# Stage o of an eight-stage network on one core: each block's product with the values issued one step later, with its transposed weights in two buffers

## The reference, cut to what matters

```python
def block(i, qb):
    sc = jnp.einsum('bqhd,bkhd->bhqk', qb, k, preferred_element_type=f32) * scale
    p = jax.nn.softmax(jnp.where(chunk_causal_mask(i, s), sc, -jnp.inf), axis=-1)
    return jnp.einsum('bhqk,bkhd->bqhd', p.astype(v.dtype), v)
```

## Time and profile before

| | us |
|---|---|
| median of 3 runs | 3006.23 |
| lowest, highest | 3006.18, 3006.42 |
| profiled execution, its own time | 3008.05 |
| its span | 3006.3 |
| PE busy in it | 2913.7 (97%) |
| DVE busy | 1715.1 (57%) |
| ACT busy | 1061.7 (35%) |
| weight transfers | 456 of 512 KB |

### The profile page before, as it was taken

One profiled execution on the slowest core, in us unless ns is written; L12 is line 12 of the kernel. 1 busy time (PEld: TensorE's weight loads), 2 busy tenths in 40 slices (PEclk: granted clock), 3 DMA queues, 4 the chain that ended last, 5 costly groups with the idle time before them and its releaser, 6 DMA issues.

```text
span 3006.3 us, 38676 instructions
## 1 busy us (share of the span) xinstructions
PE 2913.7 (97%) x14206; PEld 2406.5 (80%) x14206; DVE 1715.1 (57%) x2639; ACT 1061.7 (35%) x1601; POOL 211.6 (7%) x256
## 2 busy tenths in 40 slices
PE   8999999999999999999999999989999988999998
PEld 6888888888888888878888876588888875788887
DVE  5554535765577666654455586656444576464445
ACT  4332323543354432233332324343232345442222
POOL 1000000000000100000000000015511110110001
PEclk9999999999999999999999999989999999999999
DMA  4322232122212233333222331113332310223332
GB/s 147 98 93 89 91 106 78 57 57 78 84 57 64 70 107 98 93 97 97 92 91 91 91 99 43 29 57 113 98 95 87 105 57 22 64 84 98 93 96 91
DMA packets 70400, 252.14 MB, mean 84 GB/s; under 512 B 7808, under 2 KB 9856, under 8 KB 69632
## 3 DMA queue, kind: packets, MB, share of 16 engines
q1 hardware_dynamic: 68112, 241.89, 26.4%
q10 hardware_dynamic: 2016, 7.96, 0.8%
q0 software_dynamic: 144, 0.52, 0.0%
HBM read 248.25 MB, written 2.10 MB: 83 GB/s over the span
## 4 chain that ended last, share of the span: by engine, by line
PE 85%; DVE 8%; ACT 4%; issue 3%; POOL 1%; DMA 0%; DVEq 0%; ACTq 0%; POOLq 0%
PE ps L297 18%; PE ps L299 17%; PE ps L298 17%; PE ps L568 2%; PE ps L569 2%; PE ps L570 2%; ACT w_high L277 2%; DVE w_low L284 2%; PE ps L782 1%; PE ps L784 1%; PE ps L783 1%; PE ps L1809 1%; PE ps L855 1%; PE ps L591 1%; PE ps L841 1%
## 5 line engine op out<-in xcount | busy, mean ns | idle before, releaser
L284 DVE TENSOR_TENSOR w_low<-raw,w_high 128x1024 fp32r<-128x1024 f32 x456 | 566.4, 1247 | 417.4 <-ACT w_high L277 410.3
L297 PE MATMUL ps<-h_high,w_high 128*128 128x512 f32 x1872 | 737.1, 394 | 3.4 <-DVE arena L969 1.7
L299 PE MATMUL ps<-h_high,w_low 128*128 128x512 f32 x1872 | 729.7, 390 | 0.0
L298 PE MATMUL ps<-h_low,w_high 128*128 128x512 f32 x1872 | 729.2, 390 | 0.0
L277 ACT ACTIVATE w_high<-raw 128x1024 fp32r<-128x1024 f32 x456 | 477.9, 1051 | 448.6 <-PE ps L299 204.2
L297 PEld LDWEIGHTS ps<-h_high,w_high 128*128 128x128 f32 x1872 | 352.1, 188 | 75.1 <-DVE arena L969 2.5
L299 PEld LDWEIGHTS ps<-h_high,w_low 128*128 128x128 f32 x1872 | 351.7, 188 | 73.7
L298 PEld LDWEIGHTS ps<-h_low,w_high 128*128 128x128 f32 x1872 | 352.0, 188 | 69.7
L297 PE MATMUL ps<-y_high,w_high 128*128 128x512 f32 x640 | 250.4, 391 | 0.6 <-DVE y_low L1944 0.2
L298 PE MATMUL ps<-y_low,w_high 128*128 128x512 f32 x640 | 249.1, 389 | 0.0
L299 PE MATMUL ps<-y_high,w_low 128*128 128x512 f32 x640 | 249.0, 389 | 0.0
(11 more groups left out here) (443 smaller groups left out, 4511.0 us busy)
## 6 DMA issues: line engine op xcount, KB each, us to landing
raw<-stream SPq DMA_DIRECT2D x456, 512.0 KB, 3.6
table<-tables_in ACTq DMA_DIRECT2D x5, 1088.0 KB, 6.4
x<-x_in ACTq DMA_DIRECT2D x8, 256.0 KB, 8.3
x_out<-x SPq DMA_DIRECT2D x16, 128.0 KB, 1.7
const<-const_in SPq DMA_DIRECT2D x1, 673.0 KB, 8.0
arena<-ssm_in POOLq DMA_DIRECT2D x1, 512.0 KB, 5.9
params<-params_in ACTq DMA_DIRECT2D x1, 287.0 KB, 6.7
```

The costliest lines, as they stand in the source:

```text
L284: nc.vector.tensor_tensor(w_low[:, u.slot], raw[:, u.raw], w_high[:, u.slot].bitcast(F32), ALU.subtract).then_inc(weights_low, 1)
L297: nc.tensor.matmul(bank, wh, high[:, k], start=k == 0, stop=False)
L298: nc.tensor.matmul(bank, wh, low[:, k], start=False, stop=False)
L299: mm = nc.tensor.matmul(bank, wl, high[:, k], start=False, stop=k == tiles - 1)
```

## The change

`o_step` now gives v = n - 4, so a block's product comes one step later, and there are 28 steps instead of 27. `o_wt` becomes a pair: even blocks (128 or 384 columns) go to a region of 384 columns in the constants (the last 128 columns of the mask `chunk` and two rotation matrices), odd blocks (256 or 512 columns) to the place used before. ACT's copy of block n - 2 now waits for the product of block n - 4 (`o_pv` at tr - 1). PE's transposition of block n - 2 gets an explicit wait for ACT's copy of block n - 3 (`o_wt_copied` at tr), because bank 6 is still single. With v, the head's end moves too: `y_high` on ACT and `y_low` on DVE come one step later, in the steps with n = 4h + 7 instead of 4h + 6 for head h.

```diff
-        O_STEPS = NBLK * MLA_HEADS + 3
+        O_STEPS = NBLK * MLA_HEADS + 4
...
-        o_wt = work[:, 0:T]
+        o_wt = (con("chunk", 3 * P, 3 * P), work[:, 0:T])
...
-            s, w, t, v = (m if 0 <= m < O_BLOCKS else None for m in (n, n - 1, n - 2, n - 3))
+            s, w, t, v = (m if 0 <= m < O_BLOCKS else None for m in (n, n - 1, n - 2, n - 4))
...
                         for kb in range(b + 1):
                             mm = nc.tensor.matmul(ps[:, o_pv_bank(h), b * P:(b + 1) * P], o_v[:, kb, h * P:(h + 1) * P],
-                                                  o_wt[:, kb * P:(kb + 1) * P], start=kb == 0, stop=kb == b)
+                                                  o_wt[v % 2][:, kb * P:(kb + 1) * P], start=kb == 0, stop=kb == b)
                         mm.then_inc(o_pv, 1)
                     if tr is not None:
                         pe.wait_ge(o_scaled, tr + 1)
+                        if tr > 0:
+                            pe.wait_ge(o_wt_copied, tr)
...
-                        if tr > 0:
-                            act.wait_ge(o_pv, tr)
-                        nc.scalar.activation(o_wt[:, 0:width], ps[:, 6, 0:width], ACT.Copy).then_inc(o_wt_copied, 1)
+                        if tr > 1:
+                            act.wait_ge(o_pv, tr - 1)
+                        nc.scalar.activation(o_wt[tr % 2][:, 0:width], ps[:, 6, 0:width], ACT.Copy).then_inc(o_wt_copied, 1)
```

## The result

The kernel before took 3006.37 us in the median of 8 runs (3006.18 to 3008.39), the changed kernel 3016.11 us in the median of 8 (3013.66 to 3020.00). The ratio is 1.0032, with an interval of 1.0021 to 1.0042: slower by 0.3%, or 9.7 us. The forecast was 3007.6 us, its range ended at 3010.6, and a loss above 3012.2 had a chance of 0.03. The prediction was wrong.

A forecast was written before the change was run, and what follows sets the result against it. PE's chain of waits (85%) was taken as the bound, so only time PE loses can be won; eight nonzero or zero terms and a ninth of 0 summed to +1.42 us on 3006.23, giving 3007.6 us, range 3003.6 to 3010.6.

The forecast's parts named there:

- term 3: Step 10: DVE's `y_low` goes to step 11, so block 11's mask starts earlier: -0.33 us, bounds 0 and -0.68.
- the first rival: PE's waits for ACT's copy really go, transpositions follow earlier: in full 2998.3 us (chance 0.02), in part 3003.7 (0.26).
- term 7: Steps 22 and 23: three groups replace four at the low clock, -0.44, then four replace one, +0.67: +0.23 us.
- 1, up to `cy`: Step 3 loses block 0's product, for whose scores DVE waited; products of steps 4 to 6 lie in pauses: -0.22 us.
- 2, block 3 behind `cy`: Block 3's four groups leave the pause ahead of `cy` for step 7, where one group stood: +0.67 us.
- 4, steps 12 to 17: Pauses ended by the exponential, squares, tanh and scaling; products of any size fit into them: 0.
- 5, behind `glu`: Steps 18 and 19 follow `glu` without a pause; 3 + 4 groups where 4 + 1 stood: +0.45 us.
- 6, `y_low` at the gate: The fourth head's `y_low` comes directly ahead of the gate's tiles and delays block 19's inverse: +0.62 us, bounds 0 and +0.68.
- 8, the end: Last transposition starts slightly earlier, last product waits for ACT's copy as before: 0, at best -0.1 us.
- a rival with 0.20: PE's clock falls to low at `cy` or `glu`: one 3009.8 us (0.15); both 3012.1 (twice or with more, 0.05).
- a sign of being wrong: A granted clock of 0.50 where it was 1.00, or the reverse, would show the forecast wrong; no size given.
- The rival that a fall goes away: The mostly low-clock 7.5 us from 2559.11 shrink by at most 3.3 us: 3004.3; not expected, no separate chance given.

The follow-up runs named there:

- warm kernels: The orders before and after the change, both with unread matmuls in PE's pauses: before_warm 3004.67 us and after_warm 3006.04 us.
- before_warm: Kernel before plus unread matmuls in PE's pauses (7 ahead of `cy`; 3, 3, 6 in steps 13, 17, 21): 3004.67 us, ratio 0.9987.
- after_warm: Changed kernel plus unread matmuls in PE's pauses (7 ahead of `cy`; 5, 5, 10 in steps 13, 17, 21): 3006.04 us, ratio 0.9992.
- cy_ahead: Changed kernel with block 3's product put back into the pause ahead of `cy`: 3012.08 us, ratio 1.0008 to before.
- fill_cy: Changed kernel plus 7 unread matmuls ahead of `cy` only: 3011.76 us, ratio 1.0011 to before.
- after_again: Changed kernel run once more, unaltered, beside the kernel before: 3016.36 us, ratio 1.0021.
- behind_cy: Kernel before with the buffer pair and only block 3's product, with head 0's `y_high` and `y_low`, moved to step 7: 3013.18 us, ratio 1.0010.
- before_warm2: before_warm0 plus 2 unread matmuls in step 2 and 5 in step 25: 3000.91 us, ratio 0.9971 to the kernel before.
- before_warm0: before_warm plus 8 unread matmuls ahead of the scores of step 0: 3004.28 us, ratio 0.9987 to the kernel before.

## Why the prediction was wrong

**The waits.** Right. They moved from the products to the transpositions, 12.7 us to 1.3 and 3.9 to 13.9 of weight loads. Counted from the scores of its own block, in the warm kernels, a transposition came 0.14 to 0.23 us earlier for blocks 3, 4, 8, 12, 16, 20 and 23, and 0.60 for block 10, which `y_low` no longer holds (term 3). For the others it came at the same time or up to 0.66 later, and in sum nothing is won: the first rival is refuted. The page's rule "Double-buffer for performance" of the Trainium skill (Trainium Kernel Development and Optimization, Best Practices), carried over to this buffer, brought nothing: the pair alone is 0.9999 of before, and with the later products it costs 1.41 us at a constant clock.

**The terms of the order.** Right but for term 7 and, by 0.1 us, terms 6 and 8; before_warm against after_warm for those that the clock touches:

| term | forecast | measured | from |
|---|---|---|---|
| 1, up to `cy` | -0.22 | -0.23 | 14.37 to 14.14 us from the opening product to `cy` |
| 2, block 3 behind `cy` | +0.67 | +0.67 | warm kernels, block 6's to block 7's scores: 5.36 to 6.03 |
| 3, `y_low` out of step 10 | -0.33 | -0.34 | block 7 to 11: 17.76 to 17.42 |
| 4, steps 12 to 17 | 0 | 0 | warm kernels, block 11's to block 17's scores: 17.23 and 17.23 |
| 5, behind `glu` | +0.45 | +0.43 | transposition of block 15 to scores of block 19: 9.81 to 10.24 |
| 6, `y_low` at the gate | +0.62 | +0.52 to 0.54 | scores of block 19 to its inverse: 3.60 to 4.12 (4.14 in the warm kernels) |
| 7, steps 22 and 23 | +0.23 | +0.45 | warm kernels; the -0.44 assumed a low clock |
| 8, the end | 0, at best -0.1 | -0.10 | warm kernels: 4.33 to 4.23 |
| sum | +1.42 | +1.41 | warm kernels, whole stretch |

That the sums agree to 0.01 us is luck. Term 7 was too small by 0.22, as it took what step 22 saves at the low clock, and terms 6 and 8 made up for most of that.

(In term 2, block 6's scores start DVE at 2504.23 in before_warm and 2506.76 in after_warm, block 7's at 2509.59 and 2512.79.)

**The step that failed: the clock.** The sum took the granted clock as that of the trace before, and put its fall into a rival with 0.20 and a price of 2.2 us per place. The prediction had named a granted clock of 0.50 where it was 1.00 as a sign of being wrong, and that is what came. Three things were wrong in it.
- The chance. I judged the pause ahead of `cy` by a stretch cut at 2502 to 2504, 0.91 of 2.00 us busy. That is mostly the end of step 6's scores. In the 2.00 us right ahead of `cy` PE did nothing, before as after, and over 4 us it worked 1.99 before. So the place was thinner than the row that I took for safe, and the change made it 1.82. The clock then fell in this pause in one profiled execution, and just behind it in the other. cy_ahead shows that the product's return ends the fall, and fill_cy that unread matmuls there do. The place `glu`, named in the same rival, did not fall.
- The price at `cy`. Forecast 2.2, measured 5.28 - 2.78 = 2.5 for `cy` alone. From the start of `cy` to the scores of block 7 it is 8.94 - 5.38 = 3.56, of which the moved product is 0.67: 2.9 us.
- The falls that were there already. I held them fixed. In the first profiled execution their low clock went from 3.4 to 6.8 us and from 6.8 to 10.2; in after_again the first of them is gone and the second is 6.8, with 3.4 more from 2579. PE's pause at the gate grew as the forecast said (0.18 of 2.00 us busy became 0.00), and the four-group product of step 23 then lay in the low clock: from block 22's to block 23's scores 4.97 us, against 3.22 in after_warm. The rival that a fall goes away was priced, the one that a fall grows was not.

In all, 1.41 us are order and 6.47 are clock in the stretch of the first execution; in the second they are 1.41 and 1.16, if the order costs the same there. Outside the stretch the first lost 2.06 - 0.34 = 1.7 us net, the second 8.0, with 4.3 and 13.3 more low us there than before. The 8.0 is more than half of 13.3, so some of it is neither order nor clock, and its cause is open. So where the clock's part is lost changes from execution to execution. That it is the clock's does not rest on these two: with the pauses filled the medians of the two orders are 1.37 us apart, unfilled 9.7 and 8.5, and all 19 executions of the changed kernel have a mean granted clock of 0.982 to 0.984, where 71 of 79 of the kernel before, in the three groups, have 0.984 to 0.986. Why the changed kernel has more low us even in code ahead of the change stays open: no run separates this from the difference between executions.

**The range.** It ended at one more fall, 3010.6, which is 4.4 us above the kernel before. Even one moved product (behind_cy) gives 5.3 us in the median.

## What to carry to other kernels

Work that lies in a pause of TensorE isn't free to move: it may be what keeps the clock of the following stretch high. Before moving work out of a pause, look at PE's busy time there and at the granted clock behind it, and price a fall, and a longer one where there already is one, with a real chance when the pause is thin. Look at the microseconds that end with the pause, not at a stretch cut on a fixed grid. Where pauses can't be closed, unread matmuls that end before the wait does cost nothing on the path and can win more than the order of the work: here 8 us in the median, all places filled.

## What the runs showed of the hardware

- A low us costs 0.41 to 0.45 us in the stretch: (82.89 - 78.67) / 10.2 for the order of before, (90.77 - 80.08) / 23.8 for that of after. Ahead of it, at 2476 to 2487, it costs less: from one product of line 2218 to the next it is 16.61 us with 10.2 low us (before, from 2473.95) and 14.62 with none (before_warm2, from 2473.68), so 0.20 each. All are under the half that a low clock takes of matmuls alone. My reading is that part of it lies beside other engines' work. So the low us of a whole execution don't give its time: behind_cy has 13.8 more than before and a span only 5.1 us longer, before_warm0 6.7 fewer than before_warm and a span 0.9 us shorter.
- A fall moves easily to the next thin place: with the pause of step 0 filled it came behind the next pause, in step 2 (before_warm0), and only with both filled it stayed away (before_warm2), in one profiled execution of each.
- The same kernel shows falls of different length at one place in two executions (6.8 and 3.4 low us at `cy`), with nearly the same total. What sets the length stays open.
- The kernel before takes over 3015 us in 8 of its 79 executions of the three groups (3016.6 at most). All 8 have a mean granted clock of 0.982 or 0.983, the level of the changed kernel, where the others have 0.984 to 0.986. So they are slow by the clock too; what starts it in them is not shown.
